# Joint front of a streaming encoder step: products taken round the column groups, the gates' place and time of load, and the pieces' places in the plan

## The chip, the cores and the metric

One core of a Trainium2 chip runs the kernel as one program. The metric is device time in microseconds (us) from start to end of the program; runs before are three, and one further execution was profiled. Engines: PE is TensorE (PEld its weight loads), DVE VectorE, ACT ScalarE, POOL GpSimd, SP SyncE. All numbers are float32.

## What is computed

```
h = RMSNorm(x);  z = h @ w_in      (q, k, v of two attentions, forget logits, two gates)
o_A = DiffAttn(q_A, k_A, v_A)      8 heads, two maps a head, relative bias, chunk mask
o_B = FoX(q_B, k_B, v_B, logf)     8 heads, causal, decays from a running sum of logf
x   = x + (sigmoid(g_A) * (o_A @ w_pa) + sigmoid(g_B) * (o_B @ w_pb)) @ w_o
x   = x + PEER(RMSNorm(x))         8 heads pick 16 of 16384 experts a token
y   = RMSNorm_final(x)
```

512 prompt tokens (no past) and 32 sample tokens (with a cache of 512 past keys and values) go through one layer of width 1024. An expert is one row of 8 KB in HBM: its vector u (1024 numbers) and its vector v. A token gets, for each of its 128 picked experts, weight * gelu(u . x) times v.

## The kernel before, in words

**Tiles.** Tokens are cut in five tiles: 0 to 3 of 128 prompt tokens, 4 of 32 sample tokens. Tile 4 has no front of its own end to end: from the output projection of attention on, tiles 3 and 4 go through the matmuls together as 160 columns (WIDE). That is the joint front (JOINT = 3).

**Experts.** For a tile, 128 slots (32 for tile 4, whose tokens stand four times beside each other). A slot gathers one expert row a token, 128 rows of 8 KB, 1 MiB, by an indirect DMA that POOL issues (L761), into one of 8 places of the ring. DVE takes the dot product (L1904), ACT the gelu (L1066), and then one of two adders adds the weighted v: the "tensor" adder makes a diagonal (on DVE, L1915, or on ACT, L1078) and multiplies it with v on PE into the accumulator acc (L1512, four records a slot); the "vector" adder multiplies and adds on DVE (L1922, L1929). A place of the ring is gathered into again only when its dot product and its adder are done. Two slots make a half block: 64 half blocks a tile.

**The plan.** `make_plan` writes one list of events, and every engine walks the same list in its own instruction order. While tile t's experts run (stage t), the front of tile t + 1 goes beside them: `spread` deals its pieces over 60 half blocks in proportion to `weight_of`. A piece that comes with a half block stands behind it on PE, DVE and ACT; in attention, DVE first waits for the piece's own needs and then adds the half block's slots (`waiting`).

**A front in pieces.** f0 opens (piece 0), att0 to att13 (ATTEND; the last two steps only drain), norm and turn of o (NORM_O, TURN_O), y0 to y3 (YPROJ: w_pa and w_pb, 1.5 MiB a piece, merged with the gates on DVE, L1754 to L1757), o0 to o3 (OPROJ, 1 MiB each), norm and turn of x, q0 to q7 (QPROJ, 1 MiB each), score (1 MiB), and the eleven route pieces top0 to top10 (TOP), which run on DVE. Stage 0 carries besides the last 17 chunks of the projection of tiles 1 to 4 (project, 1 MiB each, on PE). The joint front, beside stage 2, has eight sample pieces s0 to s7 more, between TURN_O and y0: s0 loads the past logf and forms the decays, s1 to s3 score, s2 to s4 apply the values, s6 and s7 norm and turn. Weights wait in three buffers, which SP fills in order as `w_used` frees them (L724). Just before the fourth of the joint front's weights SP's queue holds `load_cache`: 4 MiB into kaT and va once heads 0 to 7 of tile 3 are done, 2 MiB into kbT and vb once all are.

**Who adds.** `beside` names what a half block has beside it, and ON_VECTOR gives its adder from that: in "project" every slot is the vector adder's, in "attend" three of eight, in "turn" and "route" none, in "nothing" three of eight.

**The sample's matmuls.** In `sample`, four heads stand below each other: head i's 32 queries are PE's output rows 32i to 32i + 31, one of four column groups. `scores` (L1312) goes round the groups and the two halves of the rows. `biases` (L1322 to L1331) and `pv` (L1360) finish one head's products before they go to the next.

**The gates.** sigmoid(g) is computed in the projection, written to HBM (`zt_mid` for tiles 1 to 3, `zt[4]` for the sample; L906, L908) and read back when a front needs it. For the joint front this is done by ACT in s7 (L966 to L969), after its last tiles of o are stored, into the front area (F): 1 MiB for tile 3 in pieces of 512 bytes and 0.25 MiB for the sample in pieces of 128 bytes. The merge waits for it (L1751). va holds keys' values [128 partitions, 5 tiles, 1024]; rows 32 to 127 of its tile 4 hold other things to the end.

## Time and profile before

| | us |
|---|---|
| median of three runs | 2258.48 |
| the three runs | 2258.48, 2267.33, 2255.89 |
| the profiled execution | 2266.87 |
| its span, first to last instruction | 2265.1 |
| PE, DVE, ACT, POOL busy in the span | 1745.0, 1465.2, 522.9, 753.6 |
| DMA | 745.10 MB, mean 329 GB/s over the span |

The span is the profile's; the profiled execution's own time has 1.8 us more around it. Stages, by the first dot product of each tile: stage 0 from 415.0, stage 1 from 943.6, stage 2 from 1340.0, stage 3 from 1836.7, stage 4 from 2175.4 us. How to read it: no engine is near its whole span, so what bounds the kernel differs by stretch, and a stretch is read by what its engines and its DMA did in it. A half block's time is the distance from its first dot product to the next half block's.

### The profile page before, as it was taken

What the parts mean: (1) busy time and instruction counts of PE and PEld (TensorE: products, weight loads), DVE (VectorE), ACT (ScalarE), POOL (GpSimd) and SP (SyncE); (2) the same over time, 40 slices, a digit from 0 to 9 for tenths busy, and PEclk for the clock granted to TensorE, in tenths of its full rate; (3) what the DMA queues carried; (4) which work ended last, traced back from release to release, by engine and by line L of the source; (5) the groups of instructions that cost most, each with busy time, mean ns of one, the idle gap of its engine ahead of it and who ended that gap; (6) DMA issues with size and microseconds to landing.
All of it is one profiled execution on the core that took longest, in us unless ns stands there. A gap on an engine that the chain in (4) does not pass through costs nothing. (4 is left out here: it accounts for less than half of the span.)

```text
span 2265.1 us, 21403 instructions
## 1 busy us (share of the span) xinstructions
PE 1745.0 (77%) x6855; PEld 1020.4 (45%) x6855; DVE 1465.2 (65%) x3305; ACT 522.9 (23%) x1438; POOL 753.6 (33%) x697
## 2 busy tenths in 40 slices
PE   7889899689977886687787779887787666566665
PEld 6855676345744772244664224434564222122211
DVE  0022207577777449898757979754548977888776
ACT  3232012121145021254012226421013210001011
POOL 0000000345433123355434444323124454555442
PEclk9999999899998898899898899879889887878887
DMA  7842555899989887799999989968778889999986
GB/s 241 295 152 75 177 194 181 333 391 406 340 341 367 345 330 268 286 379 377 421 421 420 396 363 348 414 236 339 289 284 336 327 356 407 421 422 421 421 363 275
DMA packets 130720, 745.10 MB, mean 329 GB/s; under 512 B 20496, under 2 KB 35520, under 8 KB 45104
## 3 DMA queue, kind: packets, MB, share of 16 engines
q0 software_dynamic: 78336, 570.46, 62.7%
q1 hardware_dynamic: 27712, 149.68, 18.0%
q10 hardware_dynamic: 24560, 23.58, 3.1%
q8 instruction: 55, 0.90, 0.2%
q14 instruction: 57, 0.47, 0.1%
HBM read 724.85 MB, written 18.30 MB: 328 GB/s over the span
## 5 line engine op out<-in xcount | busy, mean ns | idle before, releaser
L761 POOL DMA_INDIRECT ring<-in_uv,stage x544 | 687.2, 1263 | 1075.6 <-PE acc L1512 359.2
L1512 PE MATMUL acc<-ring,diag 128*128 128x512 f32 (+1 forms) x1252 | 706.0, 712 | 308.5 <-DVE diag L1915 218.8
L1904 DVE CUSTOM_DVE_ANT_0 ring<-ring,xb 128x1024 f32<-128x1024 f32 x544 | 649.5, 1222 | 125.3 <-DMA ring<-in_uv,stage 105.2
L1512 PEld LDWEIGHTS acc<-ring,diag 128*128 128x128 f32 (+1 forms) x1252 | 258.0, 219 | 715.6 <-DVE diag L1915 318.7
L1066 ACT ACTIVATE gel<-dots 128x1 f32<-128x1 f32 x544 | 103.3, 200 | 983.2 <-DVE dots L1904 978.0
L1929 DVE SCALAR_TENSOR_TENSOR vsum<-ring,coefd,vsum 128x1024 f32<-128x1024 f32 x226 | 290.9, 1287 | 8.1
L1184 PE MATMUL pz<-F,wbuf 128*128 128x416 f32 (+1 forms) x656 | 241.7, 528 | 12.4 <-ACT F L896 4.4
L779 POOL COPY stage<-idx 128x4 int32<-128x4 int32 x136 | 63.7, 468 | 405.7 <-DVE gw L1850 404.9
L1184 PEld LDWEIGHTS pz<-F,wbuf 128*128 128x128 f32 (+1 forms) x656 | 125.6, 194 | 124.9 <-issue 124.9
L1922 DVE TENSOR_SCALAR coefd<-gel,gw 128x1 f32<-128x1 f32 x231 | 48.6, 210 | 132.8 <-ACT gel L1066 132.2
L1184 PE MATMUL pz<-ring,wbuf 128*128 128x128 f32 (+1 forms) x656 | 81.2, 284 | 10.7 <-ACT ring L860 4.7
L1184 PE MATMUL pz<-wbuf,F 128*128 128x256 f32 (+1 forms) x384 | 85.0, 381 | 1.9 <-PE pz L1184 1.9
L1915 DVE TENSOR_SCALAR diag<-ident,gel,gw 128x128 f32<-128x128 f32 x201 | 71.4, 362 | 20.9 <-ACT gel L1066 17.9
L1184 PEld LDWEIGHTS pz<-ring,wbuf 128*128 128x128 f32 (+1 forms) x656 | 76.5, 193 | 18.0 <-issue 16.6
L1066 ACT ACT_TABLE_LOAD x56 | 71.8, 1283 | 32.8 <-DVE xb L1970 16.1
L1184 PEld LDWEIGHTS pz<-wbuf,F 128*128 128x128 f32 (+1 forms) x384 | 64.3, 170 | 22.8 <-issue 6.8
L1470 PE MATMUL pz<-F,wbuf 128*128 128x128 f32 (+1 forms) x384 | 53.9, 304 | 10.4 <-DMA wbuf<-in_w_q 8.9
L1470 PEld LDWEIGHTS pz<-F,wbuf 128*128 128x128 f32 x384 | 51.6, 209 | 12.7 <-DMA wbuf<-in_w_q 10.7
L1470 PE MATMUL ps<-F,wbuf 128*128 128x128 f32 (+1 forms) x384 | 48.7, 285 | 4.5 <-DMA wbuf<-in_w_q 2.3
L1470 PEld LDWEIGHTS ps<-F,wbuf 128*128 128x128 f32 x384 | 46.9, 191 | 7.8 <-issue 4.5
L1577 DVE TENSOR_SCALAR sst<-sst 128x1 f32<-128x1 f32 (+3 forms) x20 | 3.1, 157 | 69.1 <-ACT x L810 48.9
L1416 PE MATMUL ps<-F,wbuf 128*128 128x128 f32 (+1 forms) x192 | 31.3, 335 | 20.2 <-DVE F L1757 16.1
(373 smaller groups left out, 1863.3 us busy)
## 6 DMA issues: line engine op xcount, KB each, us to landing
wbuf<-in_w_z SPq DMA_DIRECT2D x52, 1024.0 KB
wbuf<-in_w_q SPq DMA_DIRECT2D x32, 1024.0 KB
wbuf<-in_w_pa SPq DMA_DIRECT2D x16, 1024.0 KB
wbuf<-in_w_o SPq DMA_DIRECT2D x16, 1024.0 KB
ring<-in_uv,stage POOLq DMA_INDIRECT x544
wbuf<-in_w_pb SPq DMA_DIRECT2D x16, 512.0 KB
zt_mid<-F ACTq DMA_DIRECT2D x28, 192.0 KB
wbuf<-in_w_sk SPq DMA_DIRECT2D x4, 1024.0 KB
```

Source lines behind the costliest of these rows:

```text
L761: pool.indirect_dma_start(out=ring[:, slot, :], out_offset=None, in_=d["uv"], in_offset=bass.IndirectOffsetOnAxis(ap=stage[:, a, k:k + 1], ...
L779: nc.gpsimd.tensor_copy(stage[:, a, :], idx[:, t % 2, BLOCK * b:BLOCK * b + BLOCK]).then_inc(staged[a], 1)
L1066: nc.scalar.activation(gel[:, slot:slot + 1], dots[:, slot:slot + 1], ACT.Gelu).then_inc(gelued, 1)
L1184: last = nc.tensor.matmul(out, left, right, start=(k == 0), stop=(k == KT - 1))
L1416: last = nc.tensor.matmul(banks(t)[f % 4][:, 0:n], wa[:, k, j * P:(j + 1) * P], fa(t).oaT[:, k, 0:n], start=(k == 0), stop=(k == 7))
L1470: last = nc.tensor.matmul(banks(t)[f % 4][:, 0:cols_of(t)], w[:, k, j * P:(j + 1) * P], fa(t).xbT[:, k, 0:cols_of(t)], start=(k == 0), sto ...
L1512: last = nc.tensor.matmul(acc[0:nq, c * 512:(c + 1) * 512], diag[:, parity, 0:nq], ring[:, slot, D + c * 512:D + (c + 1) * 512], start=Fal ...
L1577: nc.vector.tensor_scalar(sst[rows, a:b], sst[rows, a:b], 1.0 / width, EPS, ALU.mult, ALU.add).then_inc(ssq_mean, 1)
L1904: nc.vector.tensor_tensor_reduce(out=u, in0=u, in1=xb[:, t % 2, :], scale=1.0, scalar=0.0, op0=ALU.mult, op1=ALU.add, accum_out=dots[:, sl ...
L1915: nc.vector.tensor_scalar(diag[:, parity, 0:nq], pick[:, 0:nq], gel[:, slot:slot + 1], g, ALU.mult, ALU.mult).then_inc(coef_set, 1)
L1922: nc.vector.tensor_scalar(c, gel[:, slot:slot + 1], g, None, ALU.mult).then_inc(coefd_set, 1)
L1929: last = nc.vector.scalar_tensor_tensor(vsum[:, :], v, c, vsum[:, :], ALU.mult, ALU.add)
```

## The change

Three edits.

1. The sample's products. `pv` has its two loops exchanged: the five key tiles j outside, the four heads i inside. In `biases` the past's bias of all four heads comes before the new keys' bias; for FoX the four heads and two halves are gone round for the decays of the past, then for those of the new keys, then the causal tiles. The products are the same in number and shape.
2. The gates. The projection writes g of tile 3 and of the sample together to `zt_joint`, 160 columns a row (two DMAs a unit, as before). ACT reads it back in s4, before it stores the third and fourth turned maps, with one DMA of 1.25 MiB, 10 KB in a row in HBM and in SBUF, into the first 2560 columns of va, which by then has been read for the last time as values (pv_done of the second step has been waited for). The two DMAs of s7 and their waits go; `merge` waits for one landing.
3. The plan. `weight_of` gives the joint front's and the sample's pieces 1.0, route pieces there 1.5; in the front of tile 1 (beside stage 0) it gives y 5.0, o 3.5, q 3.0, attention 4.4; a projection chunk 11.5. What comes out, as half blocks of the stage:

| stage, pieces | before | after |
|---|---|---|
| 0, chunks 11 to 26 | 0 to 29 | 0 to 27 |
| 0, f0 and attention | 30 to 41 | 28 to 38 |
| 0, turn of o, y0 to score | 42 to 49 | 39 to 49 |
| 0, route | 50 to 59 | 50 to 59 |
| 1, all | | the same |
| 2, f0 and attention | 0 to 17, three of them without a piece | 0 to 13, one piece each |
| 2, norm and turn of o | 18, 19 | 14, 15 |
| 2, s0 to s7 | 20 to 30, three without a piece | 16 to 23 |
| 2, y0 to score | 31 to 42 | 24 to 42 |
| 2, route | 43 to 58 | 43 to 58 |

`beside` follows: in stage 2 the tensor adder has 74 slots for 84 and the vector adder 54 for 44; in the other stages the numbers stay. Stages 3 and 4 are untouched.

```diff
 def weight_of(event):
     what, i, p = event
+    if i == JOINT or what == "sample":
+        return 1.5 if what == "front" and p >= TOP else 1.0
     if what == "project":
-        return 12.0
-    if what == "sample":
-        return 5.0
+        return 11.5
+    if i == 1 and (YPROJ <= p < NORM_X or QPROJ <= p < SCORE):
+        return 5.0 if p < OPROJ else 3.5 if p < NORM_X else 3.0
+    if i == 1 and ATTEND <= p < NORM_O:
+        return 4.4
...
+        zt_joint = nc.dram_tensor("zt_joint", (P, 16, WIDE), F32, kind="Internal").ap()
...
         def gates_of(t):
-            return fa(t).gates[:, 0:16 * cols_of(t)].rearrange("p (k q) -> p k q", k=16)
+            if t == JOINT:
+                return va[:, :, :].rearrange("p a b -> p (a b)")[:, 0:16 * WIDE].rearrange("p (k q) -> p k q", k=16)
+            return fa(t).gates.rearrange("p (k q) -> p k q", k=16)
...
+                        elif kind == "g":
+                            c = (JOINT - 1) * P
+                            act.dma_start(zt_mid[0:JOINT - 1, :, k0, :].rearrange("t p q -> p t q"),
+                                          dst[:, 0, 0:c].rearrange("p (t q) -> p t q", q=P)).then_inc(z_saved[b], 16)
+                            act.dma_start(zt_joint[:, k0 - z_first["g"], :], dst[:, 0, c:n]).then_inc(z_saved[b], 16)
...
+                    if v == 2:
+                        wait_saved(act, group_of(t))
+                        act.dma_start(gates_of(JOINT), zt_joint).then_inc(gates_landed, 16)
...
-                    wait_saved(act, group_of(t))
-                    act.wait_ge(pv_done, 16 * t + 4)
-                    act.dma_start(gates_of(JOINT)[:, :, 0:P], zt[JOINT][:, 12:28, :]).then_inc(gates_landed, 16)
-                    act.dma_start(gates_of(JOINT)[:, :, P:WIDE], zt[t][:, 12:28, :]).then_inc(gates_landed, 16)
...
                 def biases(step_):
...
+                    for i, rows in at:
+                        for m, s, r in halves:
+                            nc.tensor.matmul(s[rows, 0:PAST], foxq[r, i, 0:DEC], ckey[r, 0:PAST], start=False, stop=True)
+                    for i, rows in at:
+                        for m, s, r in halves:
+                            nc.tensor.matmul(s[rows, PAST:NTOK], foxq[r, i, 0:DEC], ckey[r, PAST:NTOK],
+                                             start=False, stop=False)
...
                 def pv(u):
...
-                    for i in range(4):
-                        for j, w in ((0, P), (1, P), (2, P), (3, P), (4, DEC)):
+                    for j, w in ((0, P), (1, P), (2, P), (3, P), (4, DEC)):
+                        for i in range(4):
...
-                    dve.wait_ge(gates_landed, 16 * (t + (2 if t == JOINT else 1)))
+                    dve.wait_ge(gates_landed, 16 * (t + 1))
```

## Rows read from the trace of the kernel before

**Rows 1.** Busy by stretch: us; PE, PEld, DVE, ACT, POOL; PEclk; DMA share; GB/s.
```profile
943.60:1340.00 396.40, 307.64 (x1177) 177.00 (x1177) 319.85 (x726) 122.66 (x337) 178.71 (x160) 0.91 0.98 395
1082.20:1195.80 113.60, 91.98 (x537) 75.30 (x536) 77.03 (x144) 13.55 (x49) 43.53 (x39) 0.93 1.01 421
1340.00:1453.60 113.60, 98.23 (x396) 51.87 (x396) 100.70 (x205) 67.44 (x129) 40.22 (x41) 0.93 0.94 366
1465.50:1563.00 97.50, 79.64 (x464) 39.73 (x464) 52.86 (x107) 24.22 (x56) 24.76 (x27) 0.80 0.69 272
1563.00:1712.70 149.70, 117.75 (x646) 94.16 (x647) 73.57 (x142) 16.53 (x53) 33.09 (x33) 0.90 0.79 309
```

**Rows 2.** The same for the dot products (L1904) alone, two records a slot.
```profile
1082.20:1195.80 113.60, 33.76 (x57) 0.93 1.01 421
1340.00:1453.60 113.60, 42.62 (x72) 0.93 0.94 366
1375.57:1379.86 4.29, 2.37 (x4) 0.85 0.93 349
1465.50:1563.00 97.50, 26.16 (x44) 0.80 0.69 272
1555.92:1563.04 7.12, 2.37 (x5) 0.76 1.01 408
1563.00:1712.70 149.70, 28.56 (x49) 0.90 0.79 309
```

**Rows 3.** TensorE matmuls by line, 1465.5 to 1563 us: busy, mean ns | idle before.
```profile
L1360 PE MATMUL po<-va,F 128*32 128x128 f32 (+1 forms) x80 | 17.5, 390 | 0.0
L1360 PE MATMUL po<-vb,F 128*32 128x64 f32 (+1 forms) x80 | 6.4, 223 | 1.7 <-ACT F L948 1.7
L1327 PE MATMUL pz<-ckey,x 16*32 16x512 f32 x8 | 6.0, 916 | 0.0
L1327 PE MATMUL ps<-ckey,x 16*32 16x512 f32 x8 | 3.7, 600 | 0.0
```

**Rows 4.** Waits, 1465.5 to 1565 us: waiting <- waited for: us in total, times, longest.
```profile
DVE F L1729 <- PE po L1360: 13.0, 2, 8.0
...
DVE nmax L1734 <- PE ps L1331: 7.1, 1, 7.1
...
DVE nmax L1734 <- PE pz L1331: 5.2, 1, 5.2
```

**Rows 5.** Waits, 1563 to 1605 us, columns as in rows 4.
```profile
DVE F L1754 <- DMA F<-zt: 23.5, 1, 23.5
...
PE ps L1416 <- DVE F L1757: 16.1, 1, 16.1
```

**Rows 6.** Timeline of TensorE's matmuls: start us, us, line, operation, shapes.
```profile
1498.57 8.24 PE L1360 MATMUL po<-va,F 128*32 128x128 f32 x40
...
1508.66 0.61 PE L1312 MATMUL ps<-kbT,qT 64*32 64x512 f32 x1
...
1508.70 0.61 PE L1312 MATMUL pz<-kbT,qT 64*32 64x512 f32 x1
1509.11 0.59 PE L1312 MATMUL ps<-kbT,qT 64*32 64x512 f32 x1
```

**Rows 7.** Timeline of ScalarE where the joint gates are asked for.
```profile
1557.84 4.31 ACTq L969 DMA_DIRECT2D F<-zt  x1
1562.20 0.30 ACT L1066 ACTIVATE gel<-dots 128x1 f32<-128x1 f32 x2 [4.41 <-issue]
```

**Rows 8.** Busy time in stretches of stage 0, columns as in rows 1.
```profile
415.00:641.30 226.30, 206.44 (x708) 127.46 (x708) 153.31 (x239) 37.40 (x112) 107.50 (x78) 0.96 0.94 372
641.30:724.40 83.10, 67.92 (x274) 38.29 (x275) 67.47 (x159) 46.54 (x107) 28.81 (x30) 0.90 0.95 383
724.40:834.80 110.40, 84.33 (x499) 72.82 (x498) 52.47 (x106) 14.40 (x41) 23.92 (x21) 0.86 0.84 336
761.69:787.48 25.79, 20.50 (x97) 17.47 (x98) 8.14 (x18) 0.41 (x2) 2.59 (x3) 0.87 0.76 297
```

More of the change, by code:

```diff
@@ L390, in __init__ @@
         self.sqS = M[:, 0:256]
-        self.gates = M[:, 0:2560]
         self.mT = M[:, 0:1280].rearrange("p (k q) -> p k q", k=8)
@@ L1315, in biases @@
                 def biases(step_):
-                    for m in range(2):
-                        s = sample_bank(m)
-                        for i in range(4):
-                            rows = slice(DEC * i, DEC * i + DEC)
-                            if step_ < 2:
+                    at = [(i, slice(DEC * i, DEC * i + DEC)) for i in range(4)]
+                    if step_ < 2:
+                        for m in range(2):
+                            s = sample_bank(m)
+                            for i, rows in at:
@@ L1321, in biases @@
                                 h = 4 * step_ + i
                                 nc.tensor.matmul(s[rows, PAST - P:PAST], eye, bias[0:DEC, h, 0:P], start=False, stop=True)
+                            for i, rows in at:
+                                h = 4 * step_ + i
                                 last = nc.tensor.matmul(s[rows, PAST:NTOK], eye, bias[0:DEC, h, P:P + DEC],
                                                         start=False, stop=True)
-                            else:
-                                r = slice(32 * m, 32 * m + 16)
-                                nc.tensor.matmul(s[rows, 0:PAST], foxq[r, i, 0:DEC], ckey[r, 0:PAST], start=False, stop=True)
-                                nc.tensor.matmul(s[rows, PAST:NTOK], foxq[r, i, 0:DEC], ckey[r, PAST:NTOK],
-                                                 start=False, stop=False)
-                                b = slice(32 * m, 32 * m + DEC)
-                                last = nc.tensor.matmul(s[rows, PAST:NTOK], ident[b, b], causal[b, b], start=False, stop=True)
+                            last.then_inc(scored, 1)
@@ new lines, in biases @@
+                        return
+                    halves = [(m, sample_bank(m), slice(32 * m, 32 * m + 16)) for m in range(2)]
+                    for i, rows in at:
+                        for m, s, r in halves:
+                            nc.tensor.matmul(s[rows, 0:PAST], foxq[r, i, 0:DEC], ckey[r, 0:PAST], start=False, stop=True)
+                    for i, rows in at:
+                        for m, s, r in halves:
+                            nc.tensor.matmul(s[rows, PAST:NTOK], foxq[r, i, 0:DEC], ckey[r, PAST:NTOK],
+                                             start=False, stop=False)
@@ L1332, in biases @@
+                    for m, s, r in halves:
+                        for i, rows in at:
+                            b = slice(32 * m, 32 * m + DEC)
+                            last = nc.tensor.matmul(s[rows, PAST:NTOK], ident[b, b], causal[b, b], start=False, stop=True)
                         last.then_inc(scored, 1)
@@ L1351, in pv @@
                     pe.wait_ge(tail_stored, u + 1)
-                    for i in range(4):
-                        for j, w in ((0, P), (1, P), (2, P), (3, P), (4, DEC)):
+                    for j, w in ((0, P), (1, P), (2, P), (3, P), (4, DEC)):
+                        for i in range(4):
                             if u < 2:
```

## The prediction

> **What bounds the kernel now.** I read the busy time by stretch first. Stage 1 is the measure of a good stage: 396.4 us at 395 GB/s, and its projection stretch (y0 to score) runs at 421 GB/s for 113.6 us, which is the highest rate the rows show, so there the transfers set the pace [rows 1]. Stage 2 has the same 128 gathers and takes 1836.7 - 1340.0 = 496.7 us. The reader should see that it loses in two stretches: the sample's, at 272 GB/s, and y0 to score, at 309 GB/s, while attention has PE busy for 98 and DVE for 101 of 113.6 us [rows 1]. The dot products alone, two records a slot, tell how many half blocks a stretch got through: 18, 11 and 12 in the joint front's three, 14 in stage 1's projection [rows 2]. So 373 us for 43 half blocks up to the first route piece, 8.67 us each, where 43 gathered half blocks are some 90 MB of the 119 MB moved (41.6, 26.5 and 46.3 in the three stretches, rate by time, and some 5 between them). At 421 GB/s those bytes take 283 us: there is room.
>
> What holds the sample's stretch is PE. Four heads' products are done one head after the other: the values cost 17.5 + 6.4 us and the decays of FoX 6.0 + 3.7 us of PE [rows 3], and DVE, which stands in order with the dot products behind it, waits for just these, 13.0, 7.1 and 5.2 us [rows 4]. What holds the projection is the gates' wait: 23.5 us of DVE at L1754, behind which PE stands for 16.1 us [rows 5].
>
> **The change part by part**, against the profiled execution, 2266.9 us.
>
> (1) Products. What does going round the groups give? The rows have it for 64 row tiles: L1312's eight products start within 0.04 us of each other, and the next eight 0.45 us after the first [rows 6]. By that, four column groups cost what one did: 17.5 + 6.4 goes to 6.0, and 9.7 to 2.4 (that FoX's two row halves could go together as well I leave out). That is 25.2 us of PE. On the path lies what DVE waited for, 13.0 + 7.1 + 5.2 = 25.3, less about 2 us of plain latency in each of the four waits, so 17.3; I take **17.5**. The bounds are 0 (they don't run side by side) and 25. The bias edit is of half a us and costed at nothing; if it did nothing the loss is that. PE's granted clock is 0.80 on average in this stretch, a mix of its two levels [rows 1]; a PE with less to do may be granted less, and what PE does besides (some 54 us) would stretch: that is in the lower bound.
>
> The rows show this side-by-side start only for tiles of 64 rows, and `pv` has 128. The Trainium skill ("TensorE: Matmul & The Clock Gate", Part 3, The mechanism) says that a weight load overlaps with matmuls in flight only where the row group differs. All of pv's tiles have all rows, so by that rule `pv` would gain nothing. What the trace has is the other way for 64 rows: a second round of L1312's products on the same rows starts 0.45 us after the first, while those, 0.61 us long, still run [rows 6].
>
> (2) Attention of the joint front, 18 to 14 half blocks. Three half blocks without a piece go; the first took 4.3 us, the three together 12.8 (the first of them: [rows 2]). att0 joins f0's half block, which saves one pair of dot products, 2.4 us. Together **-15.2**. Nothing queues anew: each piece meets the same two slots as now. But the empty ones may be where PE works off its adders (1.25 tensor slots a half block, 2 us each), so the gain may be only 8; it may reach 20. The transfers cover it: four gathered half blocks fewer, 8.4 MB, from 366 GB/s. The caches' 6 MiB are asked for when tile 3's heads are done and are wanted at s1 and s3, the last six half blocks after the end of attention, as against seven now; some 35 us is enough for 2 MiB at these rates. If that cover were gone, s3 would wait up to 10 us.
>
> (3) The sample's pieces, 11 to 8 half blocks. The three empty ones, 4.1 + 4.3 + 7.1 = 15.5 us (the last of them: [rows 2]), go. In the last of them ACT stands 4.4 us in the issue of the sample's gates, 4.31 us for one DMA, and the gelus and diagonals behind it [rows 7]; that is within the 15.5. With (1) the stretch goes from 97.5 to 64.5: **-33.0**. Bounds -15 and -42.
>
> (4) y0 to score, 12 to 19 half blocks. I build this from stage 1: 14 half blocks in 113.6 us at 421 GB/s. Five more are five times 2.1 MB, 5.0 us each, so 138.5. The joint front has 160 columns and o's second set of products; PE has 118 us in this stretch now [rows 1], within 138, so most is hidden, and I add 6: 144.5 against 149.7, **-5.2**. This has the gates' wait at zero: the DMA is asked for in s4, five half blocks (25 us or more) before y0's merge, for 1.3 MB in rows of 10 KB, where now as many bytes in pieces of 512 and 128 bytes are asked for at 1557 us and waited for long after the projection has begun. If the cover is gone the wait is back up to 23.5 us. What is late next is the weights, in line with the gathers. The ten slots that go from PE to DVE cost DVE 10 x (1.5 - 0.35) = 11.5 us, in half blocks where stage 1 has DVE busy for 77 of 113.6 us: nothing on the path. Bounds: 138 (-11) and 160 (+10).
>
> (5) Moved DMAs and waits. ACT issues one DMA in s4 instead of two in s7. Its waits (all saves, pv of the second step) were met long before, so nothing queues behind them; 0.5 us of issue falls before a gelu, covered by the third step's chain. The saves of g stay two a unit. SP's and POOL's queues are passed by nothing. 0, bounds -1 and +1.
>
> (6) Stage 0. The projection chunks have 28 half blocks for 30; PE is busy 206 of 226 us there, so PE sets it, and two half blocks fewer of DVE's adders give little: -3. Attention has 11 for 12: -3. y0 to score has 11 for 8. It moved 110.4 x 336 = 37 MB and took 110 us; the four o pieces in one half block took 25.8 us with transfers at 297 GB/s [rows 8]. With three gathered half blocks more it is 43.4 MB, 103 us at 421 GB/s, 107 with some slack: -3. Together **-9**. Bounds -22 (each of the three at its floor) and +8 (attention and chunks, both near PE's limit, spill what they are given).
>
> Route (top) pieces, stage 1, 3 and 4: as before, 0. Route of stage 2 stands at the same half blocks and DVE sets it.
>
> Sum: -15.2 - 33.0 - 5.2 - 9 = -62.4, so 2204.5 for an execution like the profiled one. That one lies 8.4 us over the median of the three runs; for the median I say **2196**. The mean joint half block would go from 8.67 to 7.4 us.
>
> **The rivals.**
>
> *The products stay in line.* If a tile of all 128 rows can't have its weights loaded while another one's product runs on these rows, pv stays at 8.24 us for 40 records [rows 6] and only FoX's two row halves gain, 9.7 to 4.9 us; on the path that is some 3.5 for 17.5, 14 us less gained, **2210**. Against it is L1312's second round, on the same 64 rows. (This is what the rule of the Trainium skill named above would do.) Chance 0.12.
>
> *Packing returns nothing.* What an empty half block takes is adders' work that its neighbours left, and it comes back. Then (2) gives 8, (3) 26, (4) costs 10 and (6) is 0: -24, **2234**. For it: PE is busy for 98 of 113.6 us in attention. Against: in the empty half block of 4.3 us the dot products alone are 2.4. Chance 0.12.
>
> *Slower.* With no half block left without a piece, DVE stands in each for PE's scores or weights, and the wait is added to each. The point from which it decides is 8.67 us a half block over the 43; attention's own take 6.6 now, the projection's 12.5. At 9.0 us it is 43 x 0.33 = +14, with stage 0 at +4 it is +18: **2276**. Against it: fewer gathers stand in each stretch that PE sets and more where the transfers were idle. Chance 0.03.
>
> *No effect*, the gates' DMA late and the products in line together with the second rival: **2258**, chance 0.03.
>
> **How the numbers follow.** The forecast has the remaining 0.70. The low end is each term at its better bound, -20 -42 -11 -22 = -95, of which I take most: 2166. The high end takes in the first two rivals: 2234. About half a per cent, 11 us, is what a measurement of this kernel tells from no change. Faster by more: 0.94; within: 0.03; slower: 0.03.
>
> **What would show it.** Right: L1360 at 6 us and the L1327 rows at under 3 us of PE; no wait of L1754 for a DMA; no 4.3 us issue on ACT; the joint front's 43 half blocks in some 320 us, y0 to score at 400 GB/s or more; stage 0 shorter by some 9 us. Wrong: L1360 still at 17.5 + 6.4 us (first rival); attention's half blocks in the joint front at over 7.5 us (second); DVE's waits for PE at each piece with the rate under 320 GB/s (third); a new wait at s3 for the cache, or in the projection for w_q.

## The result, and the profile after

The changed kernel takes 2198.32 us (median of four runs, 2195.83 to 2201.74) against 2262.90 beside it: ratio 0.9717, 95% interval 0.968 to 0.9753. The forecast was 2196. The profiled execution took 2198.59 us with a span of 2196.4, so the two profiled executions differ by 68.3 us (their spans by 68.7), the medians by 64.6.

Busy time by stretch of the changed kernel, columns as in [rows 1]; the stretches are chunks, attention, y0 to score and route of stage 0, then attention, sample and y0 to score of the joint front:

```profile
410.60:622.90 212.30, 199.85 (x684) 123.82 (x685) 142.97 (x224) 36.28 (x106) 98.56 (x73) 0.97 0.91 368
622.90:702.00 79.10, 66.23 (x291) 38.44 (x290) 64.42 (x152) 43.70 (x105) 25.59 (x27) 0.96 0.94 380
702.00:825.30 123.30, 94.06 (x547) 80.17 (x545) 65.57 (x127) 15.96 (x49) 32.13 (x30) 0.86 0.93 372
825.30:927.50 102.20, 66.24 (x145) 28.02 (x144) 91.06 (x279) 22.78 (x76) 37.37 (x36) 0.87 0.78 291
1328.30:1427.70 99.40, 87.04 (x379) 48.29 (x380) 85.69 (x178) 64.50 (x120) 27.74 (x32) 0.95 0.87 336
1438.50:1502.90 64.40, 48.10 (x440) 23.61 (x440) 42.59 (x88) 22.09 (x47) 16.75 (x19) 0.76 0.80 313
1502.90:1651.50 148.60, 123.26 (x663) 98.89 (x665) 109.98 (x197) 20.61 (x72) 55.69 (x50) 0.90 0.94 387
```

Read it against [rows 1, 8] by length first: where did the 68.7 us of span come from?

| stretch (us; half blocks) | before | after | forecast for the difference |
|---|---|---|---|
| up to the first dot product | 415.0 | 410.6 | 0 |
| stage 0, chunks | 226.3 (30) | 212.3 (28) | -3 |
| stage 0, attention | 83.1 (12) | 79.1 (11) | -3 |
| stage 0, y0 to score | 110.4 (8) | 123.3 (11) | -3 |
| stage 0, route | 108.8 | 102.2 | 0 |
| stage 1 | 396.4 | 400.8 | 0 |
| joint attention | 113.6 (18) | 99.4 (14) | -15.2 |
| norm and turn of o | 11.9 (2) | 10.8 (2) | 0 |
| sample | 97.5 (11) | 64.4 (8) | -33.0 |
| joint y0 to score | 149.7 (12) | 148.6 (19) | -5.2 |
| joint route, to the end of stage 2 | 124.0 | 118.6 | 0 |
| stages 3 and 4 | 428.4 | 426.3 | 0 |

The 4.4 us before the first dot product and the 4.4 us lost in stage 1 are the spread of executions: over the 14 profiled kernels of this case the first dot product lies between 410.6 and 420.4 us and stage 1, which no edit touches, takes 396 to 404 us. The sample's stretch gives half of the gain, its rate going from 272 to 313 GB/s, and PE's busy time there falls from 79.6 to 48.1 us.

TensorE's matmuls by line from 1438.5 to 1503 us, columns as in [rows 3] (L1379 is the old L1360, L1342 the 512-column part of the old L1327):

```profile
L1379 PE MATMUL po<-va,F 128*32 128x128 f32 (+1 forms) x80 | 5.0, 420 | 0.4 <-ACT F L962 0.4
L1379 PE MATMUL po<-vb,F 128*32 128x64 f32 (+1 forms) x80 | 2.3, 268 | 2.1 <-ACT F L962 2.1
L1342 PE MATMUL ps<-ckey,x 16*32 16x512 f32 x8 | 1.1, 600 | 0.0
L1342 PE MATMUL pz<-ckey,x 16*32 16x512 f32 x8 | 1.1, 600 | 0.0
```

Count and shape are those of [rows 3], and the mean of one of the values' records is not shorter (420 ns for 390). What fell is the time in which at least one runs: 17.5 to 5.0 us and 6.4 to 2.3 for the values, 9.7 to 1.1 for the decays (the two rows of L1342 are the same 1.1 us, since `ps` and `pz` run at one time; together they are busy for 1.09 us). The timeline shows how: of FoX's products, all eight of a round (four heads, both row halves) start within 0.04 us, and the next round begins 0.45 us after the first, before that has ended.

```profile
1473.86 0.61 PE L1342 MATMUL ps<-ckey,x 16*32 16x512 f32 x1
...
1473.90 0.61 PE L1342 MATMUL pz<-ckey,x 16*32 16x512 f32 x1
1474.31 0.59 PE L1342 MATMUL ps<-ckey,x 16*32 16x512 f32 x1
...
1476.54 2.52 PE L1379 MATMUL po<-va,F 128*32 128x128 f32 x40 [0.41 <-ACT F L962]
```

The last of these rows is a step's forty records, 2.52 us for the 8.24 of [rows 6]. The waits of the same stretch, columns as in [rows 4] (L1748 and L1753 are the old L1729 and L1734):

```profile
DVE F L1748 <- PE po L1379: 6.9, 2, 3.8
...
DVE nmax L1753 <- PE ps L1350: 3.7, 1, 3.7
...
DVE nmax L1753 <- PE ps L1335: 2.1, 1, 2.1
```

The first two are the waits of [rows 4]: 10.6 us for 25.3. The third, for the bias of the first two score pieces, stood at 4.4 us before and is not in [rows 4]. No wait for the gates' transfer is left among those of the joint projection, and ScalarE's timeline has its issue at 0.36 us for the 4.31 of [rows 7]:

```profile
1484.10 0.36 ACTq L959 DMA_DIRECT2D va<-zt_joint  x1
```

### The profile page after: what moved, and what is told of

Read it like the earlier page. It is cut to its first block and busy times, and to the rows that moved or that the text cites. A ratio compares the mean times of both kernels' runs of the same rounds, so it can differ in the third digit from the quotient of the medians.

```text
span 2196.4 us, 21330 instructions
## 1 busy us (share of the span) xinstructions
PE 1690.8 (77%) x6815; PEld 1002.1 (46%) x6815; DVE 1476.4 (67%) x3315; ACT 517.7 (24%) x1435; POOL 746.8 (34%) x697
## 3 DMA queue, kind: packets, MB, share of 16 engines
q1 hardware_dynamic: 27712, 149.68, 18.2%
## 5 line engine op out<-in xcount | busy, mean ns | idle before, releaser
L767 POOL DMA_INDIRECT ring<-in_uv,stage x544 | 680.1, 1250 | 1019.5 <-PE acc L1531 326.5
L1531 PE MATMUL acc<-ring,diag 128*128 128x512 f32 (+1 forms) x1212 | 671.2, 701 | 302.9 <-DVE diag L1934 208.5
L1531 PEld LDWEIGHTS acc<-ring,diag 128*128 128x128 f32 (+1 forms) x1212 | 246.5, 216 | 689.5 <-DVE diag L1934 303.5
L1948 DVE SCALAR_TENSOR_TENSOR vsum<-ring,coefd,vsum 128x1024 f32<-128x1024 f32 x236 | 303.6, 1286 | 8.4
L1934 DVE TENSOR_SCALAR diag<-ident,gel,gw 128x128 f32<-128x128 f32 x191 | 67.8, 364 | 21.4 <-ACT gel L1076 18.2
L1194 PEld LDWEIGHTS pz<-ring,wbuf 128*128 128x128 f32 (+1 forms) x656 | 75.1, 191 | 13.9 <-issue 12.5
L1076 ACT ACT_TABLE_LOAD x54 | 69.3, 1283 | 19.9 <-DVE xb L1989 12.1
L1489 PE MATMUL pz<-F,wbuf 128*128 128x128 f32 (+1 forms) x384 | 53.9, 304 | 11.4 <-DMA wbuf<-in_w_q 10.3
L1489 PE MATMUL ps<-F,wbuf 128*128 128x128 f32 (+1 forms) x384 | 50.3, 291 | 5.7 <-DMA wbuf<-in_w_q 3.8
L1800 DVE FIND_INDEX8 F<-F 128x8 uint32<-128x128 f32 (+1 forms) x148 | 45.9, 331 | 0.0
```

Source lines behind the costliest of these rows:

```text
L767: pool.indirect_dma_start(out=ring[:, slot, :], out_offset=None, in_=d["uv"], in_offset=bass.IndirectOffsetOnAxis(ap=stage[:, a, k:k + 1], ...
L1076: nc.scalar.activation(gel[:, slot:slot + 1], dots[:, slot:slot + 1], ACT.Gelu).then_inc(gelued, 1)
L1194: last = nc.tensor.matmul(out, left, right, start=(k == 0), stop=(k == KT - 1))
L1489: last = nc.tensor.matmul(banks(t)[f % 4][:, 0:cols_of(t)], w[:, k, j * P:(j + 1) * P], fa(t).xbT[:, k, 0:cols_of(t)], start=(k == 0), sto ...
L1531: last = nc.tensor.matmul(acc[0:nq, c * 512:(c + 1) * 512], diag[:, parity, 0:nq], ring[:, slot, D + c * 512:D + (c + 1) * 512], start=Fal ...
L1800: last = nc.vector.max_index(index(j)[:, 8 * half:8 * half + 8], vals(j)[:, 8 * half:8 * half + 8], src(j))
```

## The experiments

Three parts, three questions: what is each worth, do they need each other, and what inside each does the work. All medians and ratios are against the kernel before, run in the same comparison. Stretches are named as in the table above and come from each kernel's profiled execution.

**Each part undone in the changed kernel, and each alone in the kernel before.**

Changed kernel, products as before:

```diff
-                    for j, w in ((0, P), (1, P), (2, P), (3, P), (4, DEC)):
-                        for i in range(4):
+                    for i in range(4):
+                        for j, w in ((0, P), (1, P), (2, P), (3, P), (4, DEC)):
...
-                    for i, rows in at:
-                        for m, s, r in halves:
-                            nc.tensor.matmul(s[rows, 0:PAST], foxq[r, i, 0:DEC], ckey[r, 0:PAST], start=False, stop=True)
+                    for m in range(2):
+                        s = sample_bank(m)
+                        for i in range(4):
...
+                                r = slice(32 * m, 32 * m + 16)
+                                nc.tensor.matmul(s[rows, 0:PAST], foxq[r, i, 0:DEC], ckey[r, 0:PAST], start=False, stop=True)
```

> The changed kernel with the sample's products (pv and biases) back in line, plan and gates as changed. My theory (products on the path of DVE): slower than the changed kernel by 17.5 us, so 2216; PE rows of pv back from 5.0 + 2.3 to about 24 us, DVE's waits for them back to some 13 and 12 us, s3 and s4 the two half blocks that grow. Rival (PE's time is covered by other work once the pieces are packed, and DVE would wait anyway): under 5 us, 2198 to 2203. Rival (packed, nothing covers it any more, and PE's whole 27 us lie on the path): 2225.

Changed kernel, gates as before (loaded in s7 by two DMAs from two places):

```diff
-                        act.dma_start(gates_of(JOINT), zt_joint).then_inc(gates_landed, 16)
...
+                    act.dma_start(gates_of(JOINT)[:, :, 0:P], zt[JOINT][:, 12:28, :]).then_inc(gates_landed, 16)
+                    act.dma_start(gates_of(JOINT)[:, :, P:WIDE], zt[t][:, 12:28, :]).then_inc(gates_landed, 16)
```

> The changed kernel with the gates loaded in s7 into the front area from two places, as before; products and plan as changed. y0's merge now stands two half blocks behind s7 as it did before. Theory (the wait of 23.5 us starves the projection stretch, and transfers set its pace afterwards): the wait of L1754's line for the DMA is back at 15 to 24 us, and the kernel loses 15 to 25 us against the changed one, 2213 to 2223. Rival (in the wider projection stretch the transfers make up for it, since gathers go on to land meanwhile): 0 to 8 us, with the wait in the rows but y0 to score no longer than 149 us plus 8.

Changed kernel, all of `weight_of` as before:

```diff
-    if i == JOINT or what == "sample":
-        return 1.5 if what == "front" and p >= TOP else 1.0
...
-        return 11.5
+        return 12.0
+    if what == "sample":
+        return 5.0
```

> The changed kernel with weight_of as before; products and gates as changed. Theory (the plan carries half: -15 in attention, -15.5 in the sample's empty half blocks, projection 12 half blocks in less than 149.7 us once the gates' wait is gone, stage 0 -12): what remains is products 17.5 and the gates' wait less what the transfers need anyway; 2262.9 - 17.5 - 20 = 2225, 27 us slower than the changed kernel. Rival (the plan does little, the work in it is only moved): under 8 us slower than the changed kernel, under 2206.

Changed kernel, only the weights of stage 0 as before:

```diff
-        return 11.5
+        return 12.0
-    if i == 1 and (YPROJ <= p < NORM_X or QPROJ <= p < SCORE):
-        return 5.0 if p < OPROJ else 3.5 if p < NORM_X else 3.0
-    if i == 1 and ATTEND <= p < NORM_O:
-        return 4.4
```

> The changed kernel with the weights of the front beside stage 0 and of the chunks as before (12.0, 5.0, 3.5, 1.8); the joint front's weights, products and gates as changed. Theory (my stage 0 term): 9 us slower than the changed kernel, 2207, with stage 0 at 528 us as before for 516.9. Rival (the 14 us by which the chunks' stretch was shorter came from ScalarE's DMA issues or from this one execution, not from the plan): within 3 us, 2195 to 2201, and the chunks' stretch stays near 212 us.

Then the kernel before with one part of the change each. The first has only the products going round:

```diff
+                    for j, w in ((0, P), (1, P), (2, P), (3, P), (4, DEC)):
+                        for i in range(4):
```

> The kernel before with the products alone. Theory: on the path where DVE waited, -17.5 us, 2245 against 2263. If the parts simply add, this and the undoing of the products in the changed kernel give the same number. Rival (in the loose plan the empty half blocks give PE's time back, so it was hidden in part): -5 to -10.

The second has only the gates' new place and time:

```diff
+                        act.dma_start(gates_of(JOINT), zt_joint).then_inc(gates_landed, 16)
```

> The kernel before with the gates alone. Theory: the wait of 23.5 us goes, and 4.3 us of DMA issue on ScalarE; the transfers had been idle or behind in this stretch (309 GB/s), so most of it counts: -20 us, 2243. Rival (transfers make it up): under -8.

The third has only the new weights:

```diff
+    if i == JOINT or what == "sample":
+        return 1.5 if what == "front" and p >= TOP else 1.0
```

> The kernel before with the plan alone. Theory (each removed half block without a piece is a saving whatever the rest does): attention -14, three empty half blocks -15, stage 0 -12, y0 to score not shorter since the gates' wait stays and the stretch takes in seven more half blocks: +10; in sum -31, 2232. Rival (parts depend on each other: without the quicker products the packed sample's pieces give nothing, and the gates' wait comes on top of a stretch set by transfers): -10 or less.

| part | undone: median | us worse than 2198.3 | alone: median | ratio to before (95%) | us better than 2260.4 |
|---|---|---|---|---|---|
| products | 2217.59 | 19.3 | 2246.11 | 0.9929 (0.9899 to 0.9959) | 14.3 |
| gates | 2219.59 | 21.3 | 2240.59 | 0.9909 (0.9881 to 0.9937) | 19.8 |
| plan | 2222.34 | 24.0 | 2234.63 | 0.9886 (0.9823 to 0.995) | 25.8 |
| sum | | 64.6 | | | 59.9 |
| of the plan, stage 0 | 2209.29 | 11.0 | | | |

The whole change is worth 64.6 us by the medians. The undone kernels were not measured beside the changed one but beside the kernel before, which had 2262.34 us there for 2262.90. By the ratios (the undone ones are 0.9803, 0.9837 and 0.9826) the parts are 19.5, 27.2 and 24.7 us taken out and 16.1, 20.6 and 25.8 put in, 71.4 and 62.5 in sum for the change's 64.0. So the parts add within what the intervals leave, whether put in or taken out; each difference is uncertain by some 7 us for the alone runs of the first two and more for the others, so an interplay of several us would not be seen. Each part alone is faster than the kernel before by its whole interval. The weights of stage 0 by themselves are less sure: undone, the ratio is 0.9768 (0.9715 to 0.982), and that interval overlaps the change's.

Where each part acts is in the profiles. The sample's stretch and the joint projection:

| kernel | joint attention | sample | y0 to score |
|---|---|---|---|
| before | 113.6 | 97.5 | 149.7 |
| products alone | 112.7 | 78.8 | 151.5 |
| gates alone | 112.7 | 91.1 | 133.6 |
| plan alone | 101.6 | 80.4 | 166.3 |
| all, products undone | 99.3 | 83.2 | 143.2 |
| all, gates undone | 99.4 | 62.6 | 168.5 |
| all, plan undone | 113.7 | 75.7 | 137.2 |
| all | 99.4 | 64.4 | 148.6 |

These eight kernels are all the combinations of the three parts, so each part can be read in four pairs that differ in it alone. Products take 15.4 to 18.8 us from the sample's stretch (18.7 put in alone, 18.8 taken out), and the projection behind it is 1.8 to 5.4 us longer with them in all four pairs. The gates' part takes 14.3 and 16.1 us from the projection in the old plan and 19.9 and 23.1 in the new. The plan takes 12.0 to 14.3 us from attention and 7.9 to 17.1 from the sample's stretch, and its seven more half blocks cost the projection 16.6 and 17.0 us with the gates late, 9.6 and 11.4 with the gates early. Taken together, the sample's stretch and the projection are the same with either plan, within 2 us in each of the four pairs (247.2 and 246.7 us; 230.3 and 231.1 with the products; 224.7 and 226.4 with the gates; 212.9 and 213.0 with both). What the plan saves it saves in attention, in stage 0 and in the route; the half blocks taken out of the sample's stretch come back in the projection.

The window row of the changed kernel with its gates undone, joint y0 to score, and its longest waits there:

```profile
1497.30:1665.80 168.50, 123.80 (x669) 99.82 (x671) 109.72 (x198) 20.70 (x72) 56.34 (x50) 0.87 0.89 352
```

```profile
DVE F L1767 <- DMA F<-zt: 24.9, 1, 24.9
PEld ps L1429 <- issue: 22.6, 3, 22.2
PE ps L1429 <- DVE F L1770: 22.0, 1, 22.0
```

PE's busy time in the stretch is that of the changed kernel within 1 us (123.8 and 123.3), and the stretch is 20 us longer: the whole of DVE's wait, and PE stands behind it, as in [rows 5].

**What in the products counts.** Two kernels take the change and put one half of its first edit back: only `pv` in line,

```diff
-                    for j, w in ((0, P), (1, P), (2, P), (3, P), (4, DEC)):
-                        for i in range(4):
+                    for i in range(4):
+                        for j, w in ((0, P), (1, P), (2, P), (3, P), (4, DEC)):
```

> The changed kernel with pv alone back in line (heads outside, key tiles inside); the FoX and bias products stay as changed. pv's rows go from 7.3 us of PE to 24. If PE's time on the path counts in proportion, this is two thirds of the loss of undoing all products (16.6 of 26 us of PE): 12 us, 2210. If the rule held that a product on the same rows can't run beside another one's weight load, the changed order would give nothing and this kernel would equal the changed one.

and only `biases` in line:

```diff
-                    for i, rows in at:
-                        for m, s, r in halves:
-                            nc.tensor.matmul(s[rows, 0:PAST], foxq[r, i, 0:DEC], ckey[r, 0:PAST], start=False, stop=True)
+                    for m in range(2):
+                        s = sample_bank(m)
+                        for i in range(4):
...
+                                r = slice(32 * m, 32 * m + 16)
+                                nc.tensor.matmul(s[rows, 0:PAST], foxq[r, i, 0:DEC], ckey[r, 0:PAST], start=False, stop=True)
```

> The changed kernel with the score products (FoX and bias) alone back in line; pv stays as changed. Undoing all products made the sample's stretch 83.2 us for 64.4, undoing pv alone 70.8. If the parts add, the rest, 12.4 us, is the score products', though they are only 7.5 of some 24 us of PE: DVE's maximum waits directly behind them, while pv has the next piece's distance to finish. So the stretch at 75 to 78 us and the kernel 10 to 13 us over the changed one, 2210. Rival (in line, either of them alone uncovers the other, so the parts don't add): stretch at 68 to 72.

They took 2205.59 us (ratio 0.9752, 0.9685 to 0.9819) and 2208.46 us (0.9768, 0.9736 to 0.98): 7.3 and 10.1 us worse than the changed kernel, and the sample's stretch is 70.8 and 71.9 us for 64.4. The second is what the rival had (68 to 72), not the theory (75 to 78). TensorE's lines in it, with `pv` in line,

```profile
L1379 PE MATMUL po<-va,F 128*32 128x128 f32 (+1 forms) x80 | 12.7, 309 | 0.0
L1379 PE MATMUL po<-vb,F 128*32 128x64 f32 (+1 forms) x80 | 6.4, 223 | 2.1 <-ACT F L962 2.1
```

and with `biases` in line:

```profile
L1337 PE MATMUL pz<-ckey,x 16*32 16x512 f32 x8 | 7.1, 1056 | 0.0
...
L1337 PE MATMUL ps<-ckey,x 16*32 16x512 f32 x8 | 5.0, 768 | 0.0
```

In line, the values' rows cost PE 11.8 us more (19.1 for 7.3) and the stretch 6.4; the decays' rows cost 11.0 more (12.1 for 1.1) and the stretch 7.5. The clock is in these rows too: PE's busy time in the whole stretch grew by only 7.2 us (55.3 for 48.1) and by 8.4 (56.5), which is 0.89 us of the stretch for one of PE both times. So the runs don't show that one kind is dearer than the other. The waits: DVE's maximum, which comes next, waits 6.7 and 6.1 us for the decays in line (3.7 in the changed kernel), and DVE waits 11.1 us for the values in line where the changed kernel has 6.9. The two halves give 13.9 us, and all of it in line cost 18.8; the other 4.9 stand between single profiles (by the medians it is 17.4 and 19.3), and no run says from what they come.

The step from in line to going round can also be read at one and the same granted clock, 1.00: a step's forty records with `pv` in line, and the same forty going round in the changed kernel with the weights of stage 0 as before (there L1375), each with its window (the clock is the third number from the end).

```profile
1483.80 5.36 PE L1379 MATMUL po<-va,F 128*32 128x128 f32 x40
```

```profile
1483.80:1489.16 5.36, 5.36 (x47) 3.77 (x41) 5.03 (x9) 3.88 (x8) 0.00 (x0) 1.00 1.01 371
```

```profile
1489.42 1.43 PE L1375 MATMUL po<-va,F 128*32 128x128 f32 x40
```

```profile
1489.40:1490.90 1.50, 1.50 (x51) 1.09 (x42) 1.44 (x3) 1.49 (x3) 0.00 (x0) 1.00 1.14 399
```

5.36 us and 1.43, with 276 ns for one record both times. The changed kernel's own two steps ran at a granted clock of 0.50, 2.52 us and 420 ns each, so what its rows show (17.5 to 5.0) has two clocks in it.

The decays in line took 12.1 us where [rows 3] have 9.7. The timeline of that kernel shows PE's clock falling among them:

```profile
1473.98 0.62 PE L1337 MATMUL ps<-ckey,x 16*32 16x512 f32 x1
1474.44 1.02 PE L1337 MATMUL ps<-ckey,x 16*32 16x512 f32 x1
1475.26 1.06 PE L1337 MATMUL ps<-ckey,x 16*32 16x512 f32 x1
```

Windows of it, same columns as above, with the granted clock 1.00 (2.4 GHz) to 1474.4 us and about 0.5 (1.2 GHz) from there:

```profile
1470.00:1474.40 4.40, 4.40 (x52) 1.65 (x51) 0.77 (x2) 0.25 (x2) 2.53 (x3) 1.00 0.69 222
1474.40:1480.00 5.60, 5.60 (x20) 1.49 (x19) 0.72 (x1) 2.58 (x5) 0.00 (x0) 0.51 0.98 375
1480.00:1485.00 5.00, 5.00 (x33) 1.97 (x35) 0.72 (x2) 0.00 (x0) 0.00 (x0) 0.50 0.04 15
```

PE was busy without a gap before it fell and after (4.40 of 4.40 us, then 5.60 of 5.60). A part of the decays' price in line is thus the clock's (with all products in line `ps` kept 3.7 us and `pz` took 6.6), and I can't separate it further.

**What in the gates' load counts.** Early, into va, but from the two old places in the old small pieces:

```diff
-                        act.dma_start(gates_of(JOINT), zt_joint).then_inc(gates_landed, 16)
+                        act.dma_start(gates_of(JOINT)[:, :, 0:P], zt[JOINT][:, 12:28, :]).then_inc(gates_landed, 16)
+                        act.dma_start(gates_of(JOINT)[:, :, P:WIDE], zt[t][:, 12:28, :]).then_inc(gates_landed, 16)
```

> The changed kernel, gates into va's place in s4 as changed, but from the two old places with two DMAs in pieces of 512 and 128 bytes, not one run of 10 KB. If the early issue is what counts: no wait of the merge for the DMA, and the loss is ScalarE's issue of the 128 byte pieces, 4.3 us, now in the middle of s4's chain: the sample's stretch at 67 to 70 for 64.4, the kernel 3 to 6 us over the changed one, 2203. If the size of the pieces counts as well: the merge waits again, 10 us or more, 2212 and up.

2201.33 us (2197.44 to 2204.6), ratio 0.9728 (0.9699 to 0.9757): 3.0 us worse, within what the intervals leave. No wait for the gates is in its profile. Its ScalarE timeline has the two issues:

```profile
1479.97 0.65 ACTq L953 DMA_DIRECT2D va<-zt_mid  x1
1480.65 4.69 ACTq L954 DMA_DIRECT2D va<-zt  x1
```

1 MiB in 512 byte pieces is issued in 0.65 us, 0.25 MiB in 128 byte pieces in 4.69, and the sample's stretch is 70.1 us for 64.4. So the early time is enough by itself to end the wait, and then the shape of the transfer is worth no more than the issue on ACT. Whether the shape would have been enough by itself, late in s7, no run tries, and the traces speak for it. The landing times (the last number, us from issue) with the gates undone, and then early in small pieces:

```profile
F<-zt_mid ACTq DMA_DIRECT2D x1, 1024.0 KB, 11.7
F<-zt ACTq DMA_DIRECT2D x1, 256.0 KB, 38.5
```

```profile
va<-zt_mid ACTq DMA_DIRECT2D x1, 1024.0 KB, 7.9
va<-zt ACTq DMA_DIRECT2D x1, 256.0 KB, 8.7
```

It is the sample's quarter MiB that the merge waits for. The trace has it as 2048 packets of 128 bytes; tile 3's 1 MiB, whose pieces are 512 bytes in SBUF, it has as 128 packets of 8 KB. Early, when the gathers moved only 1.31 MB in 21 us, the small packets began within 2.9 us; late, beside the gathers' packets of 8 KB, they took 29.0 us, and in the kernel before 29.5, half of them in the last 4.3. The large packets, issued at 1498.2 us with the gates undone, had landed by 1509.9, and DVE began to wait at 1512.6. Rows of 10 KB asked for late might thus have come in time or nearly so (they landed in 7.3 us early). That is an estimate from these rows; of the gates' 21 us the share of the time and that of the shape are not told apart.

**Room for the turned x.** In the changed kernel the transfers stop once in the joint projection, behind norm and turn of x. Windows, same columns:

```profile
1581.50:1589.90 8.40, 2.26 (x5) 0.67 (x4) 7.27 (x20) 3.08 (x6) 1.43 (x2) 0.73 0.88 366
1589.90:1596.40 6.50, 6.45 (x21) 4.11 (x22) 5.25 (x9) 1.76 (x5) 0.00 (x0) 0.55 0.00 1
1596.40:1605.60 9.20, 9.05 (x59) 8.03 (x58) 5.11 (x9) 1.09 (x5) 4.90 (x6) 1.00 0.70 234
```

If the pieces are too dense there, an empty half block should pay. Two kernels put room in. The first behind both norm and turn of x:

```diff
     if i == JOINT or what == "sample":
-        return 1.5 if what == "front" and p >= TOP else 1.0
+        if what == "front" and p in (NORM_X, TURN_X):
+            return 2.0
+        return 1.3 if what == "front" and p >= TOP else 1.0
```

> The changed kernel with norm and turn of x of the joint front at 2.0 and route pieces at 1.3: one half block without a piece behind each of the two, taken from the route pieces. In the changed kernel the transfers stand still behind turn of x (365, 1 and 235 GB/s in three half blocks), since ring and weight buffers are full while the chain of norm, root, turn runs. Theory: two more half blocks of dot products in this gap free four places of the ring; the route stretch, which DVE sets, has two half blocks less, 2 x 2.3 us, and y0 to score gets longer by less than that: 3 to 6 us faster than the changed kernel, 2193. Rival (the projection stretch is set by transfers, so each half block more costs its 5 us there): 4 us slower, 2202.

The second behind the turn alone:

```diff
     if i == JOINT or what == "sample":
-        return 1.5 if what == "front" and p >= TOP else 1.0
+        if what == "front" and p == TURN_X:
+            return 2.0
+        return 1.4 if what == "front" and p >= TOP else 1.0
```

> As the other one, but a half block without a piece behind turn of x alone, route pieces at 1.4. Theory: half the gain, 2 to 3 us, 2196; if the gap is closed by one half block, as much as two give. Rival: 2 us slower.

2204.35 us (0.9725, 0.9699 to 0.9751) and 2201.29 us (0.9722, 0.9698 to 0.9746), no better than the change: the theory of both missed. With two more half blocks the projection takes 156.9 us (148.6) and the route 90.5 (95.6); with one more, 151.9 and 92.7. Against the changed kernel's profile each costs 3 to 4 us and returns 2.5 to 3. The changed kernel's is a long projection for its plan, though (below), so the cost may be higher. I found no version that beats the changed kernel.

## Why the prediction held, point by point

**(1) Products, 17.5 forecast, 18.7 and 18.8 measured in the sample's stretch** (of the whole kernel 14.3 to 19.5, since the projection takes some back). The way taken, what DVE waits for less the latency of each wait, was sound, and its close hit is in part luck. With products alone the waits of [rows 4] went from 25.3 to 10.4 us, 14.9 less for the 17.3 forecast: 2.6 us a wait stays and not 2. Two waits that the sum left out made up for it: DVE's 2.1 us for the values at L1724, which is gone, and 4.4 us for the bias, which became 3.4. PE lost 23.0 us of busy time (79.6 to 56.6) for 25.2 forecast. FoX's two row halves, which the forecast left out, went together: 9.7 to 1.1 us for the 2.4 forecast. And the remark that a PE with less to do may be granted less fits the changed kernel, with 0.76 in the stretch for 0.80, its two steps of `pv` at 0.50 costing 2.52 us each for the 1.43 of the rows at 1.00.

The first rival (in line) is out. The rule of the Trainium skill ("TensorE: Matmul & The Clock Gate", Part 3, The mechanism) would have left `pv` at 17.5 us, since its tiles all hold all rows; the trace differs, 80 records in 5.0 us with the same shapes, and 1.43 us for 5.36 at one clock. What the runs show in its place is that tiles of the same 128 rows in different column groups run side by side. PE's weight loads of one step of `pv` are, in the changed kernel,

```profile
1476.54 1.48 PEld L1379 LDWEIGHTS po<-va,F 128*32 128x32 f32 x32 [0.53 <-ACT F L962]
```

thirty-two loads in 1.48 us, all within the products' 2.52 us. (The other eight loads are those of the 32 row tiles.)

**(2) Joint attention, -15.2 forecast, -14.2 measured.** Every kernel with the new plan has 99.0 to 101.6 us there, every one with the old 112.7 to 113.7. The second rival, that packing returns nothing, gave 8 here, and falls as a whole (2234 us). For the three half blocks of the sample's stretch its reason was right, see (4). The cache did not come late: no wait for its transfer stands among those of the sample's stretch.

**(3) Sample, -33.0 forecast, -33.1 measured.** More than half of it by products (18.7, products alone), and the rest by three half blocks fewer and the gates' issue: 78.8 to 64.4 us, 14.4 for the 15.5 that stood in the sum. ScalarE's 4.3 us issue was said to be within these; gates alone take 6.4 us from the stretch in the old plan, and the small pieces give 5.7 back in the new. With the gates undone in the new plan the stretch is 62.6 us all the same: it ends at 1497.3, the issue (5.25 us) starts at 1498.9, and the wait stands in the next one too. DVE's wait for the past logf, asked for in s0, is 3.5 to 5.4 us in every profile, before and after; no edit touches it.

**(4) y0 to score, -5.2 forecast, -1.1 measured; 148.6 us for 144.5.** The forecast has two large parts in it: the gates' wait gone (23.5 us) and the cost of seven more half blocks, which is what remains, 18.3. Measured, they are 14.3 to 23.1 and 9.6 to 17.0. So what (3) booked as 15.5 for the empty half blocks is given back here, in the forecast and in the runs alike, and a reader of (3) alone would credit the plan with it wrongly. The five other profiles with this plan in the joint front and early gates have 143.2 to 146.6 us, and rates up to 401 GB/s (the small early pieces) for the 387 of the change, so the profiled execution of the changed kernel is at the slow end. The forecast of at least 400 GB/s was a little high. Built from stage 1, the term left out the transfers' stop behind norm and turn of x, 6.5 us at 1 GB/s above; the room kernels could not get it back. The gates' wait went to zero, and is 24.9 us with the gates undone, where 23.5 was said to return if the cover is gone.

**(5) Moved DMAs, 0 forecast.** Nothing is queued anew that a profile shows. One thing I had not counted: the saves of g in the projection cost ScalarE 25.2 us of issue before and 20.5 with `zt_joint`. But the changed kernel with the old places has 22.8, and the difference lies in one to three issues of 2 to 6 us among 32, so it may not be the place's; no run says whether it is on the path.

**(6) Stage 0, -9 forecast; -11.8 between the two profiles, -11.0 by medians.** The sum is close and its terms are not. Means over the nine profiles with the new plan there and the five with the old one, new less old:

| stage 0 | forecast | measured |
|---|---|---|
| chunks | -3 | 212.1 - 223.9 = -11.8 |
| attention | -3 | 81.9 - 82.3 = -0.4 |
| y0 to score | -3 | 114.7 - 110.0 = +4.7 |
| route | 0 | 103.1 - 108.2 = -5.1 |

For the chunks I had said that PE sets them and that two half blocks fewer give little. That holds as far as it goes: PE's last chunk ends 218.5 to 222.6 us after the start of stage 0 in the old plan and 213.7 to 220.4 in the new, 2.5 us less on the mean. What I did not read is the handover behind it. TensorE's timeline of the kernel before, the last chunk first, has

```profile
623.45 14.17 PE L1184 MATMUL pz<-wbuf,F 128*128 128x256 f32 x64 [0.34 <-PE pz L1184]
644.00 5.74 PE L1512 MATMUL acc<-ring,diag 128*128 128x512 f32 x8 [6.38 <-DVE diag L1915]
649.67 0.70 PE L1213 MATMUL ps<-kaT,qT 64*128 64x256 f32 x4
```

and that of the changed kernel, the last chunk first,

```profile
614.29 14.17 PE L1194 MATMUL pz<-wbuf,F 128*128 128x256 f32 x64 [0.31 <-PE pz L1194]
...
629.66 1.98 PE L1531 MATMUL acc<-ring,diag 128*128 128x512 f32 x4 [1.20 <-DVE diag L1934]
...
634.79 0.70 PE L1223 MATMUL ps<-kaT,qT 64*128 64x256 f32 x4 [3.14 <-DVE x L1688]
```

From the last chunk's end to attention's first score is 12.1 us before and 6.3 after (11.8 to 12.5 in the five profiles with the old plan there, 6.3 in all nine with the new); the first score comes 8.3 us sooner on the mean, and the rest of the 11.8 is that DVE reaches f0's half block, where this stretch ends, before PE is through with the chunks now (212.3 for 217.9 us), and reached it after that in the kernel before (226.3 for 222.6). The plan before has one more half block without a piece between the two. No run tried that by itself; it is read from the traces. In the route, q6, q7, score and the first two route pieces had stood close together: the first two route pieces' half block took 18.2 us in the kernel before. Part of those 5.1 us is thus only moved across the border from y0 to score. The step that failed is one and the same: I priced the half blocks added and removed and not the seams between kinds of pieces. That the sum came out at -11 to -12.6 for -9 is luck: the chunks' stretch gave four times its term, and y0 to score moved the other way.

**The rest.** From the first route piece to the end of stage 2 it is 5.4 us less, forecast at 0; the part behind the route has 25.8 to 28.8 us in the kernels with the old joint plan and 23.0 to 27.5 with the new. I have no cause for it. The 43 half blocks of the joint front's three stretches and the two between took 323.2 us for 372.7, 7.5 us each (7.4 forecast). The third rival needed over 8.67. The fourth, no effect, is outside the interval. That the median lies within 2.3 us of the forecast is closer than the terms were: they missed by up to 8.8 us one way and 7.7 the other, and the route of stages 0 and 2, put at nothing, gave 6.6 and 5.4.

## What to carry to other kernels

Where several small matmuls write different column groups, put the loop over the groups innermost; the count and shape of instructions stay, and here 33.6 us of busy TensorE became 8.4, and the stretch 18.8 us shorter. Value such a gain by what the waiting engine stands for, every wait of it, and take the latency that stays in each from the rows (2.6 us here); PE's whole busy time in the stretch was as fair a measure here (23.0 and 18.1 us less for 18.7 and 18.8). When work is dealt out over a pipeline's slots, price a slot separately in each stretch and look at the seams between stretches: seven half blocks moved out of attention and the sample's pieces saved 29 us there (plan alone) and cost the projection 17. Before moving a transfer earlier, look at its packets: here 0.25 MiB in the smallest ones set the wait, and not the 1 MiB beside it.

## What the runs showed of the hardware

- Tiles of 128 rows and 32 columns in four column groups run side by side in float32: forty records of one step in 1.43 us going round the groups and in 5.36 one group after another, both at a granted clock of 1.00.
- A transfer in 2048 packets of 128 bytes (0.25 MiB) landed in 8.7 us with few other transfers under way and in 35.6, 38.5 and 43.3 us beside gathers in 8 KB packets; 1 MiB in 128 packets of 8 KB issued just ahead of it landed in 7.9 and in 10.8 to 11.7.
- The same small transfer cost ScalarE 4.31 to 5.25 us of issue in five kernels, the 1 MiB ahead of it 0.65 and the 1.25 MiB in rows of 10 KB 0.36. No run issues it without the other just ahead, so what part that has is not shown.
- TensorE's granted clock fell from 2.4 to 1.2 GHz amid a run of products without a gap, and a 512 column product went from 0.62 to 1.06 us. What set it off isn't told apart here.
